# Expert rows added on GpSimd, the last chunk's rows turned one half-chunk earlier, and the last norm and its stores divided anew

## The reference

```
logits = h @ w_router                       # 256 x 8
top_w  = softmax(top_k(logits, 2))          # two experts per token
for e in range(8):
    y = (silu(h @ w_gate[e]) * (h @ w_up[e])) @ w_down[e]     # 1024 -> 3584 -> 1024
    out = out + combine[:, e] * y
x = h + out                                 # h: residual rows
result = x * rsqrt(mean(x * x) + eps) * w   # last norm
```

## Time and profile before

| | |
|---|---|
| median of 3 runs (lowest, highest) | 1526.06 us (1525.02, 1526.5) |
| the profiled execution's own time | 1525.12 us |
| its span, first to last instruction | 1523.2 us |
| mean granted clock of TensorE | 0.997 of full speed |
| busy: PE, PEld, DVE, ACT, POOL | 99%, 83%, 79%, 64%, 10% |

### The profile page before, as it was taken

How to read it: one execution, slowest core, us unless ns; L and a number is a source line. 1 busy time by engine, 2 the same in 40 slices (tenths; PEclk the granted TensorE clock), 3 DMA queues, 4 the chain that set the end, 5 groups by cost and what they waited for, 6 DMA issues and landing times.

```text
span 1523.2 us, 22266 instructions
## 1 busy us (share of the span) xinstructions
PE 1501.9 (99%) x8266; PEld 1260.9 (83%) x8266; DVE 1210.7 (79%) x955; ACT 977.1 (64%) x802; POOL 146.0 (10%) x159
## 2 busy tenths in 40 slices
PE   9999999999999999999999999999999999999997
PEld 7888888889998888888888888888888888888885
DVE  7765555557884678888888888888889888888988
ACT  6544334445554357777777777777777777777774
POOL 1021000002242129200000000000000000000100
PEclk9999999999999999999999999999999999999999
DMA  9349655545321239999999999999999999999993
GB/s 365 124 141 401 222 190 193 193 146 185 122 85 49 99 109 357 422 403 391 371 381 391 369 371 401 375 365 394 378 380 381 376 376 380 391 372 361 423 397 120
DMA packets 91372, 455.07 MB, mean 299 GB/s; under 512 B 8000, under 2 KB 8512, under 8 KB 48320
## 3 DMA queue, kind: packets, MB, share of 16 engines
q1 hardware_dynamic: 84272, 431.11, 74.6%
q0 software_dynamic: 5904, 21.50, 3.5%
q10 hardware_dynamic: 1152, 1.83, 0.3%
HBM read 438.68 MB, written 15.73 MB: 298 GB/s over the span
## 4 chain that ended last, share of the span: by engine, by line
PE 94%; DVE 2%; DMA 1%; ACT 1%; issue 1%; POOL 0%; SPq 0%; DVEq 0%; POOLq 0%
PE PS L356 28%; PE PS L358 28%; PE PS L357 28%; PE PS L1605 2%; PE PS L1975 2%; DMA w_raw<-in_a_w_qkv 1%; DVE w_low L348 1%; PE PS L1334 1%; PE PS L1308 0%; PE PS L1585 0%; PE PS L2027 0%; ACT w_high L344 0%; PE PS L1323 0%; PE PS L1566 0%; PE PS L1482 0%
## 5 line engine op out<-in xcount | busy, mean ns | idle before, releaser
L348 DVE TENSOR_TENSOR w_low<-w_raw,w_high 128x2048 fp32r<-128x2048 f32 x405 | 927.5, 2293 | 193.0 <-ACT w_high L344 192.3
L344 ACT ACTIVATE w_high<-w_raw 128x2048 fp32r<-128x2048 f32 x405 | 776.0, 1918 | 288.7 <-PE PS L358 284.9
L356 PE MATMUL PS<-w_high,x_high 128*128 128x512 f32 x1264 | 501.3, 397 | 4.3 <-DVE w_low L348 2.0
L358 PE MATMUL PS<-w_high,x_low 128*128 128x512 f32 x1264 | 493.2, 390 | 0.0
L357 PE MATMUL PS<-w_low,x_high 128*128 128x512 f32 x1264 | 492.3, 390 | 0.0
L356 PEld LDWEIGHTS PS<-w_high,x_high 128*128 128x128 f32 x1264 | 237.4, 188 | 54.9 <-DVE w_low L348 4.9
L358 PEld LDWEIGHTS PS<-w_high,x_low 128*128 128x128 f32 x1264 | 237.2, 188 | 50.8
L357 PEld LDWEIGHTS PS<-w_low,x_high 128*128 128x128 f32 x1264 | 237.5, 188 | 46.9
L356 PE MATMUL PS<-w_high,m_act_high 128*128 128x512 f32 x448 | 175.0, 391 | 1.6 <-DVE m_act_low L2796 1.6
L358 PE MATMUL PS<-w_high,m_act_low 128*128 128x512 f32 x448 | 174.4, 389 | 0.0
L357 PE MATMUL PS<-w_low,m_act_high 128*128 128x512 f32 x448 | 174.4, 389 | 0.0
(11 more groups left out here) (330 smaller groups left out, 1242.5 us busy)
## 6 DMA issues: line engine op xcount, KB each, us to landing
w_raw<-in_m_w_blocks SPq DMA_DIRECT2D x336, 1024.0 KB, 7.0
w_raw<-in_b_w_in SPq DMA_DIRECT2D x16, 1024.0 KB, 5.4
w_raw<-in_f_w_gate SPq DMA_DIRECT2D x14, 1024.0 KB, 5.1
w_raw<-in_f_w_up SPq DMA_DIRECT2D x14, 1024.0 KB, 5.0
w_raw<-in_f_w_down SPq DMA_DIRECT2D x14, 1024.0 KB, 4.9
x_slots_dram<-zeros POOLq DMA_DIRECT2D x12, 512.0 KB, 10.4
w_raw<-in_a_w_qkv SPq DMA_DIRECT2D x5, 1024.0 KB, 12.7
w_raw<-in_a_w_o SPq DMA_DIRECT2D x4, 1024.0 KB, 15.7
```

The source lines that it names most:

```text
L344: nc.scalar.activation(WH[:, n % SPLIT, :], W[:, n % RAW, :], ACT.Copy).then_inc(hi_done, 1)
L348: nc.vector.tensor_tensor(WL[:, n % SPLIT, :], W[:, n % RAW, :], WH[:, n % SPLIT, :].bitcast(f32), ALU.subtract).then_inc(lo_done, 1)
L356: nc.tensor.matmul(o, sH, mH, start=first, stop=False)
L358: return nc.tensor.matmul(o, sL, mH, start=False, stop=last)
```

## The change

PE, ACT and DVE take step 54 out of the loop. In it PE's `down` runs the transposes of chunk 55 between its two halves; ACT and DVE read them out before their last split, into a free part of `x_high` and `x_low` (`lastH`, `lastL`), since `m_act_high` and `m_act_low` still serve the second half. `last_down` reads from there.

The adds of `yg` move from DVE to POOL, right behind the gathers: each of DVE's four instructions becomes a `tensor_scalar` (row times weight, in place) and a `tensor_tensor` (added to `h`), with a wait for each before the next. DVE keeps the copy of `pickZ` and a count on `added`, which `last_back` now waits for.

The last norm: DVE first multiplies the first 512 columns of both token tiles by `w` (without rstd), ACT then scales these by rstd; DVE does the other 512 columns of each tile as before. Stores: tile 0 in one piece of 512 KB from SP; tile 1 in two of 256 KB, one from ACT's queue and one from SP's.

```diff
+lastH, lastL = xH[:, 0:4, 128:256], xL[:, 0:4, 128:256]
 @@ sync: stores
-for t in range(TT):
-    for b in range(2):
-        sp.wait_ge(sem("fin_done"), 2 * t + b + 1)
-        sp.dma_start(out_v[:, t, CH * b:CH * b + CH], fin[:, t, CH * b:CH * b + CH]).then_inc(sem("stored"), 16)
-sp.wait_ge(sem("stored"), 16 * 2 * TT)
+sp.wait_ge(sem("fin_scaled"), 1)
+sp.wait_ge(sem("fin_done"), TT + 1)
+sp.dma_start(out_v[:, 0], fin[:, 0]).then_inc(sem("stored"), 16)
+sp.wait_ge(sem("fin_done"), TT + 2)
+sp.dma_start(out_v[:, 1, CH:D], fin[:, 1, CH:D]).then_inc(sem("stored"), 16)
+sp.wait_ge(sem("stored"), 16 * 3)
 @@ gpsimd: behind the gathers of yg
+pool.wait_ge(sem("yg_in"), 16 * 2 * TT)
+pool.wait_ge(sem("pick_done"), 2)
+for t in range(TT):
+    for c, weight in enumerate((w0, w1)):
+        link(nc.gpsimd.tensor_scalar(yg[:, c, t], yg[:, c, t], weight[:, t:t + 1], None, ALU.mult))
+        link(nc.gpsimd.tensor_tensor(h[:, t], h[:, t], yg[:, c, t], ALU.add))
+        pool.sem_inc(sem("added"), 1)
 @@ scalar: step (DVE's step is changed in the same way)
     split_high(act, n0 + 10, q)
+    if final:
+        turned(q + 1, lastH)
     split_high(act, n0 + 11, q)
 @@ scalar: after the last squares
+for t in range(TT):
+    act.wait_ge(sem("fin_done"), t + 1)
+    act.wait_ge(rstd_done, TT * norm_no["fin"] + t + 1)
+    nc.scalar.activation(fin[:, t, 0:CH], fin[:, t, 0:CH], ACT.Copy, scale=rstd[:, norm_no["fin"], t:t + 1]).then_inc(sem("fin_scaled"), 1)
+act.wait_ge(sem("fin_scaled"), TT)
+act.dma_start(out[0].rearrange("(t p) d -> p t d", p=128)[:, 1, 0:CH], fin[:, 1, 0:CH]).then_inc(sem("stored"), 16)
 @@ tensor: down, last_down, last_back, step
 for half in range(2):
+    if half == 1 and between is not None:
+        between()
     pe.wait_ge(lo_done, n + half + 1 + r * RAW)
...
-last = mm3(PS[:, 2 + b, :], maH[:, f, :], maL[:, f, :], wh[:, ff, CH * b:CH * b + CH],
+last = mm3(PS[:, 2 + b, :], lastH[:, f], lastL[:, f], wh[:, ff, CH * b:CH * b + CH],
...
-pe.wait_ge(sem("added"), 1)
+pe.wait_ge(sem("added"), 4 * LAST)
...
+def last_turned():
+    pe.wait_ge(sem("m_act_done"), E * NC)
+    turned()
...
-with pe.Fori(LAST * NC + 1, E * NC - 1) as q:
+with pe.Fori(LAST * NC + 1, E * NC - 2) as q:
     step(q)
+step(E * NC - 2, between=last_turned)
 pick_turned(1)
-pe.wait_ge(sem("m_act_done"), E * NC)
-turned()
 @@ vector: behind the last step
-turned(E * NC - 1)
-pick_turned(0, pickZ)
+dve.wait_ge(sem("pickT_ps"), 1)
+link(V.tensor_copy(pickZ[:], PS[:, 7, 0:256].rearrange("p (t c) -> p t c", t=TT)))
+dve.sem_inc(sem("added"), 4 * LAST)
...
-dve.wait_ge(sem("yg_in"), 16 * 2 * TT)
-for c, weight in enumerate((w0, w1)):
-    for t in range(TT):
-        if c:
-            dve.wait_ge(sem("added"), t + 1)
-        V.scalar_tensor_tensor(out=h[:, t], in0=yg[:, c, t], scalar=weight[:, t:t + 1], in1=h[:, t],
-                               op0=ALU.mult, op1=ALU.add).then_inc(sem("added"), 1)
-dve.sem_inc(sem("added"), 4 * LAST)
 @@ vector: last norm
 for t in range(TT):
+    dve.wait_ge(ss_done, TT * n + t + 1)
+    V.tensor_tensor(fin[:, t, 0:CH], h[:, t, 0:CH], w_fin[:, 0:CH], ALU.mult).then_inc(sem("fin_done"), 1)
+for t in range(TT):
     dve.wait_ge(rstd_done, TT * n + t + 1)
-    for b in range(2):
-        c = slice(CH * b, CH * b + CH)
-        V.scalar_tensor_tensor(out=fin[:, t, c], in0=h[:, t, c], scalar=rstd[:, n, t:t + 1], in1=w_fin[:, c],
-                               op0=ALU.mult, op1=ALU.mult).then_inc(sem("fin_done"), 1)
+    V.scalar_tensor_tensor(out=fin[:, t, CH:D], in0=h[:, t, CH:D], scalar=rstd[:, n, t:t + 1], in1=w_fin[:, CH:D],
+                           op0=ALU.mult, op1=ALU.mult).then_inc(sem("fin_done"), 1)
```

More of the change, by code:

```diff
@@ L1155, in silu, with turned @@
                     nc.scalar.activation(mg[:], PS[:, 0, :], ACT.Silu).then_inc(sem("m_silu_done"), 1)
-                def turned(q):
+                def turned(q, high=maH[:]):
                     act.wait_ge(sem("m_turn_ps"), q + 1)
-                    nc.scalar.activation(maH[:], PS[:, 4, :].rearrange("p (f q) -> p f q", f=4), ACT.Copy)\
+                    nc.scalar.activation(high, PS[:, 4, :].rearrange("p (f q) -> p f q", f=4), ACT.Copy)\
                         .then_inc(sem("m_high_done"), 1)
@@ L1173, in y_high, with step @@
                         .then_inc(sem("ys_high"), 1)
-                def step(q, out_of=None, x_of=None):
+                def step(q, out_of=None, x_of=None, final=False):
                     split_high(act, n0 + 6, q)
@@ L1199, in experts @@
                     step(j * NC + NC, out_of=j)
-                with act.Fori(LAST * NC + 1, E * NC - 1) as q:
+                with act.Fori(LAST * NC + 1, E * NC - 2) as q:
                     step(q)
-                turned(E * NC - 1)
+                step(E * NC - 2, final=True)
                 act.wait_ge(sem("jobs_done"), 1)
@@ L1976, in turned, with down @@
                     last.then_inc(sem("m_turn_ps"), 1)
-                def down(n, r, first, last_chunk):
+                def down(n, r, first, last_chunk, between=None):
                     for half in range(2):
+                        if half == 1 and between is not None:
+                            between()
                         pe.wait_ge(lo_done, n + half + 1 + r * RAW)
@@ L2040, in up, with step @@
                     gate_up(n, r, 1).then_inc(w_used, 1)
-                def step(q, first=False, final=False, x_of=None, x_wait=None, out_of=None):
+                def last_turned():
+                    pe.wait_ge(sem("m_act_done"), E * NC)
+                    turned()
+                def step(q, first=False, final=False, x_of=None, x_wait=None, out_of=None, between=None):
                     pe.wait_ge(sem("m_silu_done"), q + 1)
@@ L2054, in step @@
                         pe.wait_ge(sem("ys_out"), out_of + 1)
-                    down(n0 + 8, q, first, final)
+                    down(n0 + 8, q, first, final, between)
                 pe.wait_ge(sem("gather_low"), 1)
@@ L2792, in gated, with turned, step @@
                     V.tensor_tensor(ma[:], PS[:, 1, :], mg[:], ALU.mult).then_inc(sem("m_act_done"), 1)
-                def turned(q):
+                def turned(q, high=maH[:], low=maL[:]):
                     dve.wait_ge(sem("m_high_done"), q + 1)
-                    V.tensor_tensor(maL[:], PS[:, 4, :].rearrange("p (f q) -> p f q", f=4), maH[:].bitcast(f32),
+                    V.tensor_tensor(low, PS[:, 4, :].rearrange("p (f q) -> p f q", f=4), high.bitcast(f32),
                                     ALU.subtract).then_inc(sem("m_low_done"), 1)
-                def step(q, x_of=None):
+                def step(q, x_of=None, final=False):
                     split_low(dve, n0 + 6, q)
@@ L2808, in step @@
                     split_low(dve, n0 + 10, q)
+                    if final:
+                        turned(q + 1, lastH, lastL)
                     split_low(dve, n0 + 11, q)
@@ L2822, in experts @@
                 picks(LAST, slice(0, 128))
-                with dve.Fori(LAST * NC + 1, E * NC - 1) as q:
+                with dve.Fori(LAST * NC + 1, E * NC - 2) as q:
                     step(q)
-                turned(E * NC - 1)
-                pick_turned(0, pickZ)
+                step(E * NC - 2, final=True)
+                dve.wait_ge(sem("pickT_ps"), 1)
+                link(V.tensor_copy(pickZ[:], PS[:, 7, 0:256].rearrange("p (t c) -> p t c", t=TT)))
+                dve.sem_inc(sem("added"), 4 * LAST)
                 dve.wait_ge(sem("jobs_done"), 1)
                 njobs = dve.value_load(jobs[0:1, NJ:NJ + 1], min_val=E, max_val=JOBS)
-                dve.wait_ge(sem("yg_in"), 16 * 2 * TT)
-                for c, weight in enumerate((w0, w1)):
-                    for t in range(TT):
-                        if c:
-                            dve.wait_ge(sem("added"), t + 1)
-                        V.scalar_tensor_tensor(out=h[:, t], in0=yg[:, c, t], scalar=weight[:, t:t + 1], in1=h[:, t],
-                                               op0=ALU.mult, op1=ALU.add).then_inc(sem("added"), 1)
-                dve.sem_inc(sem("added"), 4 * LAST)
                 last_y_low(0)
```

## The result

The changed kernel takes 1529.68 us (median of 8 runs, 1528.31 to 1531.07), the one before 1525.54 (8 runs): a ratio of 1.0027, 95% interval 1.0018 to 1.0036. It is slower by 4.1 us; 5.15 were forecast. The two profiled spans, 1528.1 and 1523.2 us, differ by 4.9. Three marks on PE cut that up: the transposes of chunk 50, those of chunk 54 and the first matmul of `last_down`.

What follows compares the result with a forecast made beforehand. PE's matmuls were taken to bound the kernel, with DVE nearly full beside them in the last expert. -1.75 + 7.2 - 0.3 = +5.15 us on 1526.06 gave 1531.2 us, range 1523.4 to 1534.2.

Steps and rivals of the forecast that it cites:

- What bounds the kernel: Whole kernel: PE busy 1501.9 of 1523.2 us; edits win only where PE stands still, and DVE is nearly full beside it.
- Part 1: Last turn between the halves of `down`: transposes go in earlier, so PE starts `last_down` 1.75 us sooner.
- rival c: Tail: the turn gains nothing, its 1.75 us are lost while GpSimd's blocking stays; 1533.0 us, chance 0.05.
- Part 2: Four adds leave DVE: no gain by themselves, but otherwise they would hold `last_y_low` by 1.75 us.
- Part 3: Eight wide GpSimd operations in the last expert's full stretch block DVE's splits by turns; PE loses 7.2 us.
- neither starves: GpSimd and DVE in the full stretch: a waiting GpSimd operation enters between back-to-back splits, so the two alternate.
- the signs: From 1436 to 1470 us: splits of 3.2 and 4.5 us by turns, PE waits for `w_low` summing near 7.
- Rival a: Full stretch: nobody blocks DVE, splits stay near 2.3 us; 1524.0 us, 0.13% faster, chance 0.20.
- rival b: Full stretch: GpSimd gets in only when DVE is idle, costing 3.6 us; 1527.6 us, chance 0.12.
- Rival d: Full stretch: scalings are slow too, 1.8 us, with adds of 2.7, costing 12.3; 1536.3 us, chance 0.05.
- The single row: At 370.24 us a pair of DVE splits took 5.62 us instead of 4.58 beside a 128x1024 GpSimd operation.
- Part 4: Last norm and stores: between 0.3 us lost and 0.65 gained, taken as 0.3 us gained.

Runs made afterwards that it cites:

- turn_dve: The changed kernel with the four adds back on DVE, behind its copy of pickZ, and no GpSimd operations: 1526.24 us, ratio 1.0002 to the kernel before.
- gp_only: The kernel before with only GpSimd's eight operations added and DVE's four adds removed; turn, last norm and stores as before: 1532.22 us, ratio 1.0046.
- gp_spaced: The changed kernel with the same eight GpSimd operations, one pair in each of chunks 51 to 54: 1526.66 us, ratio 1.0002 to the kernel before.
- adds_only: The changed kernel without GpSimd's four scalings, for time alone: 1529.94 us, ratio 1.003 to the kernel before.
- spread_oldnorm: The changed kernel with the adds on DVE, one in each of steps 51 to 54, and the old last norm and stores: 1523.86 us, ratio 0.9983 to before.

## Why the prediction was right, point by point

- *What bounds the kernel*: held. DVE nearly full beside a full PE was the row that decided; a wait taken out of the tail and put into the stretch is what happened.
- *Part 1, the turn*: 1.75 forecast, 1.74 measured, and by the steps named. `last_down` began right behind the pick matmuls; the last split (done at 1512.93) lay 0.7 us ahead of need; no PE wait followed (rival c falls).
- *Part 2*: held. turn_dve began `y_last_low` at 1511.85, 0.6 later than before, and gained nothing that its time shows.
- *Part 3*: the mechanism held (gp_only, gp_spaced), and the term was 7.2 where 6.07 came. Three things differ. The scalings were taken for 1.03 long and 0.93 of blocking; they are 2.8 long and block 0.85. The pair came to 7.53 instead of 7.6. And the last scaling waited for two splits, not one: it lasted 6.78 us, so the fourth pair let three splits through in 9.5 us, 1.1 over PE's pace instead of 1.9. With that, 3 x 1.94 + 1.1 - 1.0 of slack = 5.9. Why the fourth waited twice is open. It does so again in gp_only (6.78). In the changed kernel it was the only one with another split right behind the first, but that is not enough: the scaling at 1452.61 of gp_spaced had one too and got in (4.82). So "neither starves" held, while strict turns did not. Of the signs, the 4.5 us splits came; the others took 2.60 and not 3.2, and the waits on record make 4.2 and not 7.
- *Rival a* (nobody blocks) and *rival b* (only in idle gaps, 3.6): fall by the splits of 4.4 to 4.5 us and by adds_only's splits back to back. *Rival d* (scalings of 1.8, adds of 2.7, 12.3) was nearer on the scaling's length, which is 2.8, and wrong on the price, since a scaling's length isn't what blocks. The single row on which the forecast stood was right for the adds; for the scalings, a length of 1.03 and a blocking of 0.93 were assumed, and that the blocking came near is luck, as it was taken from a length that was wrong. The counter-row, a 128x8 operation that delayed nobody, may be the same fact as the scaling's 0.85, that what counts is how long an operation reads; no run tests that.
- The rule of the Trainium skill (SBUF — State Buffer, Who interferes with whom) has the port kept for the whole instruction. The add agrees (about 2.1 of 2.34), the scaling doesn't (0.85 of 2.84); the measurement decides.
- *Part 4* is the step that failed: forecast -0.3, measured +0.17 against the profile of before, and +0.5 to +1.1 against the two other runs with the old norm (16.51, 16.62; the changed norm 17.12 to 17.57). The delay was foreseen, as two on `ms` and `rstd` together worth 0.6; it fell on `ms` alone, and the first store was 0.66 later. The 0.3 chosen let the closed gap in the stores outweigh it, and that gap was partly one slow issue of one execution: from the first store's issue to the end the changed kernel saves 0.49 on the profile of before, but only 0.1 on the two others with the old norm. The choice failed; the bound named beside it, the end up to 0.3 past where it was, held against the profile of before only.
- *The sum*: +5.15 forecast. By the marks it is 6.07 - 1.74 + 0.17 = 4.5, the medians say 4.1. The two errors, 1.1 too much in part 3 and 0.5 too little in part 4, went against each other and made the sum look better than its terms.

## What to carry to other kernels

Before work goes to GpSimd because it is idle, look at what DVE does in the same microseconds: if those are instructions with two SBUF inputs and DVE has little idle time, the time for which GpSimd's wide operations keep it out is paid by DVE, and beyond its slack by whoever waits for it: nearly the whole of a two-input add, under a third of a scaling. Look for a row of before in which the two overlap, and for one of the same operation: the one pair here priced the adds, while the scaling, of which no row stood, lasted 2.8 times what was assumed. If the work must be there, give it the moments when DVE reads PSUM (1.87 us lost here instead of 6.07); better, give DVE the cheaper fused instruction (1.28 us here against 2.8 + 2.3) in a gap of its own (0.04 lost).

## What the runs showed that was not expected

- GpSimd's `tensor_scalar` on 128x1024 fp32 takes 2.8 us by a per-partition value or by a constant (2.84, 2.77), longer than its two-input add (2.34) and 2.7 times a copy (1.04), yet holds DVE up for only 0.85.
- A 128x1 operation on GpSimd can take 1.01 us instead of 0.27 when DVE's products with two SBUF inputs run, nearly four times as long, on the path of the last norm.
- A waiting GpSimd operation gets in between two back-to-back splits of DVE, but not always at the first chance: one scaling let a split go past (6.78 us), in two kernels.
- The issue of one and the same store took 0.59, 0.63 and 1.00 us in three executions (spread_oldnorm, gp_only, before); the one with 1.00 ended 0.4 to 0.5 later than the others, counted from `last_down`.
